# Hybrid diffusion backbone on one core: one of two groups of modulation pieces multiplied and summed on VectorE beside the projection, heads turned inside the context attention, six early gathers

## The reference, cut to what matters

```
def modulation(cvec, w_mod, b_mod):
    m = jax.nn.silu(cvec) @ w_mod + b_mod      # (1024,) @ (1024, 6144) + (6144,)
    return jnp.split(m, 6, axis=-1)
...
for i in range(DEPTH):
    mx = modulation(c, w_mod[i], b_mod[i]); mc = modulation(c_ctx, w_mod[i], b_mod[i])
    hx = modulate(rmsnorm(x, norm1[i]), mx[0], mx[1])
    hc = modulate(rmsnorm(h, norm1[i]), mc[0], mc[1])
    aq, ak, av, bq, bk, bv = split_cols(h @ w_in, EVEN_SIZES)   # then rmsnorm of q and k, rope
    ...                                  # attention, merge, out projection
    x = x + mx[5] * peer(...)            # 128 gathers of p_u and p_v rows per 128 tokens
```

## Time and profile before

| | us |
|---|---|
| median of 3 executions | 4426.19 (4411.77 to 4430.12) |
| the profiled execution, its own time | 4407.58 |
| its span in the profile | 4406.3 |
| TensorE busy | 3757.3 (85%) |
| VectorE busy | 2603.1 (59%) |
| ScalarE busy | 1746.1 (40%) |
| GpSimd busy | 1689.1 (38%) |
| mean granted clock of TensorE | 0.962 |

### The profile page before, as it was taken

How to read it: one execution, slowest core, us unless ns; L and a number is a source line. 1 busy time by engine, 2 the same in 40 slices (tenths; PEclk the granted TensorE clock), 3 DMA queues, 4 the chain that set the end, 5 groups by cost and what they waited for, 6 DMA issues and landing times. The chain is left out here.

```text
span 4406.3 us, 44443 instructions
## 1 busy us (share of the span) xinstructions
PE 3757.3 (85%) x12678; PEld 1911.6 (43%) x12678; DVE 2603.1 (59%) x5667; ACT 1746.1 (40%) x5137; POOL 1689.1 (38%) x1350
## 2 busy tenths in 40 slices
PE   5988789899998899878999966787989997877787
PEld 2444644555554445433444422556444552222222
DVE  3524687667866855676644433436766558666554
ACT  1112255555554444443333322322664433333333
POOL 0100144444444443444545412001444534656665
PEclk9989999999999999999999987899999999999999
DMA  4255899999999999999999971028999999999998
GB/s 174 108 212 198 288 424 401 412 419 424 404 425 426 426 420 426 427 391 427 427 427 427 427 295 37 4 86 297 394 372 412 425 423 405 427 427 427 427 427 363
DMA packets 248572, 1562.74 MB, mean 355 GB/s; under 512 B 30851, under 2 KB 44963, under 8 KB 77190
## 3 DMA queue, kind: packets, MB, share of 16 engines
q0 software_dynamic: 185088, 1342.36, 73.1%
q1 hardware_dynamic: 61014, 213.99, 12.9%
q10 hardware_dynamic: 2224, 3.55, 0.2%
HBM read 1551.43 MB, written 8.36 MB: 354 GB/s over the span
## 5 line engine op out<-in xcount | busy, mean ns | idle before, releaser
L2823 PE MATMUL ps<-ring,ex_diag 128*128 128x512 f32 x5120 | 2476.7, 618 | 416.6 <-ACT ex_diag L2812 389.7
L1586 POOL DMA_INDIRECT ring<-in_p_uv,expert x1280 | 1633.8, 1276 | 2179.3 <-PE ps L2823 1447.4
L2787 DVE SCALAR_TENSOR_TENSOR ring<-ring,H 128x1024 f32<-128x1024 f32 x1280 | 1557.5, 1225 | 1084.0 <-DMA ring<-in_p_uv,expert 1041.2
L2823 PEld LDWEIGHTS ps<-ring,ex_diag 128*128 128x128 f32 x5120 | 923.9, 194 | 1663.6 <-ACT ex_diag L2812 847.5
L2806 ACT ACTIVATE ex_act_w<-ex_dots 128x1 f32<-128x1 f32 x1280 | 258.1, 202 | 1471.4 <-DVE ring L2787 1465.2
L2812 ACT ACTIVATE ex_diag<-ident_sb,ex_weight 128x128 f32<-128x128 f32 x1280 | 513.9, 402 | 91.6 <-issue 3.1
L2808 ACT ACTIVATE ex_weight<-ex_act_w,gates 128x1 f32<-128x1 f32 x1280 | 377.1, 295 | 91.3 <-issue 4.2
L532 PE MATMUL ps<-win_w,hT 128*128 128x512 f32 (+1 forms) x480 | 191.9, 557 | 1.9 <-PEq L283 1.4
L532 PEld LDWEIGHTS ps<-win_w,hT 128*128 128x128 f32 x480 | 90.3, 191 | 106.0 <-issue 103.9
L1945 PEld LDWEIGHTS ps<-hTc,bs_w 128*128 128x128 f32 x768 | 110.8, 191 | 29.3 <-issue 23.5
L1945 PE MATMUL ps<-hTc,bs_w 128*128 128x128 f32 (+1 forms) x768 | 120.3, 310 | 0.3 <-issue 0.3
(11 more groups left out here) (456 smaller groups left out, 3314.6 us busy)
## 6 DMA issues: line engine op xcount, KB each, us to landing
ring<-in_p_wqk SPq DMA_DIRECT2D x64, 576.0 KB, 4.8
bs_w<-in_p_wqk SPq DMA_DIRECT2D x64, 576.0 KB, 8.0
ca_mod_w<-in_w_mod SPq DMA_DIRECT2D x24, 1024.0 KB, 9.5
ring<-in_p_uv,expert POOLq DMA_INDIRECT x1280, 13.9
win_mod_w<-in_w_mod SPq DMA_DIRECT2D x16, 1024.0 KB, 4.8
bs_w<-in_e_w_out_tiles SPq DMA_DIRECT2D x24, 512.0 KB, 8.0
win_w<-in_e_w_in SPq DMA_DIRECT2D x9, 1024.0 KB, 8.9
mod_mod_w<-in_w_mod SPq DMA_DIRECT2D x8, 1024.0 KB, 14.8
```

Of the source, the lines that this page charges most:

```text
L1586: pool.indirect_dma_start(m.ring[:, r, :], None, a["p_uv"], bass.IndirectOffsetOnAxis(ap=m.expert[:, t % 2, slot % SLOTS:slot % SLOTS + 1] ...
L2787: dve.scalar_tensor_tensor(out=ring[:, r, 0:D], in0=ring[:, r, 0:D], scalar=1.0, in1=h_of(t + t0), op0=ALU.mult, op1=ALU.mult, accum_out=d ...
L2823: mm = pe.matmul(mix_banks(t)[:, half, :], diag[:, b, :], ring[:, r, D + half * BANK:D + (half + 1) * BANK], start=(n == 0), stop=(n == SL ...
```

## The change

There are four edits.

- Group 2 of layer 0's modulation leaves TensorE. The new class `ModulationSums` has VectorE multiply each 128 x 2048 piece by the stream's coefficient (one a partition) and add it to an accumulator of the same size, for both streams: 16 instructions and as many drains, two after each of the VectorE steps 2, 5, ... 23 (`SUM_AT, SUM_GAP = 2, 3`). TensorE sums the accumulators over the partitions with eight matmuls against `m.sel` after unit 27. ScalarE issues the eight loads and four bias loads; the piece's buffer and the accumulators lie in `Hn`. One buffer: each load waits for both additions of the piece before. `Modulation` in this stage keeps group 1 alone, 8 pieces, `MOD_AT` is still 14, so they follow units 14 to 21.
- `turn_heads` is gone as a stage. The new class `Turns` turns the 8 parts of the context tiles at the start of the context attention, in eight banks, and TensorE waits for all their copies. The 16 parts of the latent tiles are turned at slots 3 + 6 n and copied by ScalarE at slots 5 + 6 n, all through PSUM bank 1; part n waits for the copy of part n - 1.
- The modulation in the context attention has bank 0 alone, so the first piece of a group waits for VectorE's four additions of the group before, and its 24 pieces are spread over the first 88 slots of 102.
- `EARLY` goes from 4 to 6, in both layers. `w_q` keeps three buffers in ring slots 6 and 7 and gets its fourth in memory of its own.

The core of the diff:

```diff
+class ModulationSums:
+    COLS = 4
...
+    def load(self, queue, k):
+        if k:
+            queue.wait_ge(self.used, 2 * k)
+        queue.dma_start(self.w, self.a["w_mod"][self.layer, self.group, k]).then_inc(self.loaded, 16)
...
+    def add(self, eng, k, stream):
+        coef, acc = self.m.csil[:, k, 2 + stream:3 + stream], self.acc[stream]
+        eng.wait_ge(self.loaded, 16 * (k + 1))
+        if k == 0:
+            add = eng.tensor_scalar(acc, self.w, coef, None, ALU.mult)
+        else:
+            add = eng.scalar_tensor_tensor(out=acc, in0=self.w, scalar=coef, in1=acc, op0=ALU.mult, op1=ALU.add)
+        add.then_inc(self.used, 1)
+        eng.drain()
+
+    def reduce(self, pe):
+        pe.wait_ge(self.used, 2 * KC)
+        for stream in range(2):
+            for j in range(self.COLS):
+                part, _ = self.chunk(j)
+                mm = pe.matmul(self.m.ps[part, self.bank, :], self.m.sel[:, 2 * stream:2 * stream + 2],
+                               self.acc[stream][:, j * BANK:(j + 1) * BANK], start=(stream == 0), stop=(stream == 1))
+        mm.then_inc(self.reduced, 1)
...
-    MOD_AT = NU - mods.pieces
+    MOD_AT = NU - 2 * mods.pieces
+    SUM_AT, SUM_GAP = 2, 3
...
+                    if u == NU - 3:
+                        on_dve.reduce(pe)
...
+                on_dve.load(act, 0)
                 for u in range(NU):
+                    if u > SUM_AT and (u - SUM_AT) % SUM_GAP == 2 and (u - SUM_AT) // SUM_GAP + 1 < KC:
+                        on_dve.load(act, (u - SUM_AT) // SUM_GAP + 1)
...
+                    if u >= SUM_AT and (u - SUM_AT) % SUM_GAP == 0 and (u - SUM_AT) // SUM_GAP < KC:
+                        for stream in range(2):
+                            on_dve.add(dve, (u - SUM_AT) // SUM_GAP, stream)
...
                 for g in range(len(mods.groups)):
                     mods.vector(dve, g)
+                on_dve.vector(dve)
...
                 mods.store(pool)
+                on_dve.store(pool)
...
+class Turns:
...
+    def begin_tensor(self, pe):
+        for n, part in enumerate(self.first):
+            self.turn(pe, part, n).then_inc(self.turned, 1)
+        for q in range(2):
+            pe.wait_ge(self.copied[q], len(self.first) // 2)
...
+    def tensor(self, pe, slot):
+        for n in self.at["turn"](slot):
+            if n:
+                pe.wait_ge(self.rest_copied, n)
+            self.turn(pe, self.rest[n], self.bank).then_inc(self.rest_turned, 1)
...
-        mods = Modulation(m, a, s, 1, [0, 1, 2], 8, (0, 1))
+        mods, turns = Modulation(m, a, s, 1, [0, 1, 2], 8, (0,)), Turns(m, s, 1)
...
-        steps = [slots * n // mods.pieces for n in range(mods.pieces)]
+        steps = [(slots - 14) * n // mods.pieces for n in range(mods.pieces)]
...
-EARLY = 4
+EARLY = 6
...
-                    pre, mods = InWeights(m, a, s), Modulation(m, a, s, 0, [1, 2], 2, (4, 5))
+                    pre, mods = InWeights(m, a, s), Modulation(m, a, s, 0, [1], 2, (4,))
...
-                turn_heads(nc, m)
```

More of the change, by code:

```diff
@@ L169, in vector @@
             part, _ = self.chunk(g, j)
-            dve.tensor_tensor(self.row[part, g % 2], self.m.ps[part, self.banks[g % 2], :], self.bias[part, g % 2], ALU.add)\
+            dve.tensor_tensor(self.row[part, g % 2], self.m.ps[part, self.banks[g % len(self.banks)], :], self.bias[part, g % 2], ALU.add)\
                 .then_inc(self.row_ready, 1)
@@ L465, in prefetch, with project_heads @@
             self.load(sp, n)
-def project_heads(nc, m, a, pre, mods):
+def project_heads(nc, m, a, pre, mods, spare):
     ORDER = pre.ORDER
@@ L491, in project_heads @@
     with Stage(nc, "ph0") as s:
+        on_dve = ModulationSums(m, a, s, "dve", 0, 2, spare[:, 2, :], [spare[:, n, :] for n in range(2)], 5)
         sq, ss = s.sb("sq", [P, 2, BANK]), s.sb("ss", [P, 2, 8])
@@ L633, in _ @@
                 mods.store(pool)
[L636 to L665, removed]
@@ L873, in _ @@
             def _(pe):
+                turns.begin_tensor(pe)
                 for slot in range(slots):
@@ L877, in _ @@
                             mods.tensor(pe, n)
+                    turns.tensor(pe, slot)
                     for h in heads:
@@ L882, in _ @@
             def _(dve):
+                turns.begin_copy(dve, dve.tensor_copy, 1)
                 for slot in range(slots):
@@ L898, in _ @@
             def _(act):
+                turns.begin_copy(act, act.copy, 0)
                 for slot in range(slots):
+                    turns.scalar(act, slot)
                     for h in heads:
@@ L1602, in first_choice @@
     with Stage(nc, f"fc{layer}") as s:
-        w_o = m.ring[:, 0:EARLY, :].rearrange("p r d -> p (r d)").rearrange("p (k d) -> p k d", d=D)
-        w_q = m.ring[:, EARLY:, :].rearrange("p r d -> p (r d)")[:, 0:RING * (KC + 1) * P].rearrange("p (r d) -> p r d", r=RING)
+        w_o = m.ring[:, 0:KC // 2, :].rearrange("p r d -> p (r d)").rearrange("p (k d) -> p k d", d=D)
+        behind = m.ring[:, EARLY:, :].rearrange("p r d -> p (r d)")
+        w_q = [behind[:, r * (KC + 1) * P:(r + 1) * (KC + 1) * P] for r in range(RING - 1)] + [s.sb("w_q", [P, (KC + 1) * P])]
         gate, gain, scale, shift_row = (s.sb(x, [P, D]) for x in ("gate", "gain", "scale", "shift_row"))
```

73 lines of the change are left out of this document (65 added, 8 removed).

## The result

| | us |
|---|---|
| before, median of 20 executions | 4411.07 (4402.62 to 4431.52) |
| after, median of 20 executions | 4428.27 (4421.99 to 4443.7) |
| ratio, with its 95% interval | 1.0041 [1.0031, 1.0051] |
| span of the profiled execution after | 4431.2 |
| mean granted clock of TensorE after | 0.963 |

The kernel became 17 us slower, where 26 us less were forecast. The front of the kernel came out nearly as predicted; the time was lost where the prediction had said that nothing would change.

The account below looks back on a forecast made before the run. It took gather bytes to bound the two expert stages and something else the front. Terms -23.8 + 2 - 4.9 + 1 = -25.7, say -26, from 4426.2 gave 4400 us; range 4392 to 4408, with rivals 4380 to 4416.

Parts of the forecast that it names:

- The step that failed: Two expert stages: limited by the bytes their gathers move, so a change ahead shifts them without changing their length.
- the sign that would refute it: Expert stages: the prediction is wrong if they change their length by more than 5 us.
- The projection: Projection stage: seven pieces fewer on TensorE, eight reduction matmuls more; end at 272 against 285.67, 13.7 us earlier.
- the "slower" rival: Projection: VectorE becomes the bound; TensorE stands from additions of 3.6 us, 4438 at 6 us; chance 0.03.
- The turns' start: Start of context attention: turns stage goes, first piece at 278.3 against 302.07, 23.8 us earlier, the projection's 13.7 contained.
- Inside the context attention: Context attention: added turns, bank waits and thinner tail +8, higher clock 6 back; sum +2, bounds -6 and +12.
- The tail: Last value of context attention to first_choice: only copy and stage end remain, 1.9 us against 6.76, 4.9 us earlier.
- EARLY: Seam into the experts: two more gathers move the stage end back 4.9 us; +1 for both layers, bounds +9.8 and -8.
- The experts' end stay: Expert stages: with two more early gathers the idle 4 us of DMA move along unfilled, so byte count and end stay.
- the two bounds: Early gathers: +9.8 if the delay shows in both layers, -8 if the stage end waits for something else, gaps filled.
- The whole: Whole kernel: -23.8 + 2 - 4.9 + 1 = -25.7, say -26, giving 4400; chance 0.62.
- The low clock in there: Context attention: first 20 us at 0.6 clock, bank wait whole; +12 in place of +2, time 4410; chance 0.17.

## Why the prediction was wrong, point by point

**The step that failed** is the one that was taken without a price: "they are limited by the bytes that their gathers move, and a change ahead of them shifts them without changing their length". Their limit is bytes at a rate, and the rate was taken as fixed. It depends on where the ring lies, and a tensor of 16 bytes ahead of it in the list of allocations moved the ring by 32. Measured alone, this is +43 us, of at most 52; in the changed kernel it is 44 (4428.27 - 4383.98). That -26 + 43 gives just the +17 that was measured is partly luck: the edits by themselves brought 27 to 32, and the place cost 44 to 46 on top of them. The prediction named the sign that would refute it ("if the expert stages change their length by more than 5 us"), and the stages changed by 34; it had no rival and no chance for it. The row to look at was in the list of allocations and not in the trace: the diff's core, as I had cut it, left the line with `m.sel` out.

The Trainium skill has a rule near this one, page "DMA: Bandwidth & Descriptors", section "How a descriptor splits into AXI transactions": a DMA descriptor (here one row) is cut into transactions of 256 bytes, and each must start on a 256-byte boundary; when the descriptor starts elsewhere, its first transaction starts at the boundary below, and the bytes in between cost beats (of 32 bytes) too. By it a row of 8192 bytes that starts 32, 64 or 128 bytes behind a boundary takes 33 transactions in place of 32 (3%), and 257, 258 or 260 beats in place of 256 (0.4, 0.8 and 1.6%; counting the thirty-third transaction as a full one would give 264, 3%). All of these are estimates by the page. That the boundary is at 256 agrees with the runs. The size doesn't: measured are 1.6, 1.4 and 1.2% for the three distances, less than the transactions and not growing as the beats. And the page speaks of what a descriptor reads, not of the place in SBUF, the memory on the chip, that it writes. Shown is that the ring's place decides, and that 32, 64 and 128 bytes off are slow where 0, 256 and 512 are not; why is open.

**The projection: right.** Last unit's end at 272.6 for 271.2, first turn at 273.31 for 272, where 1.4 us of the difference is there from unit 8 on (115.50 for 114.06), ahead of any piece. It is older than the stage: the projection's first matmul is at 72.34 for 70.67. Of these 1.7 us, 0.8 are there when the first transposes of the normalised tiles begin (56.53 for 55.74), and 0.9 are the last group of these, which took 1.97 us for 1.10; none of it is in an instruction that the change touches. TensorE never waits for VectorE in the projection. The additions, VectorE by line and form:

```profile
L216 DVE SCALAR_TENSOR_TENSOR Hn<-Hn,csil 128x2048 f32<-128x2048 f32 x14 | 32.9, 2349 | 0.9
L214 DVE TENSOR_SCALAR Hn<-Hn,csil 128x2048 f32<-128x2048 f32 x2 | 2.6, 1286 | 0.2
```

2.35 us, for 2.29 taken from another operation of that size; the "slower" rival needed 3.6 to begin. The 13.7 us forecast for the stage were measured as 12.4 from 285.67 to 273.31, 13.8 without those 1.4; as 13.6 at the first piece of the context attention against the kernel without the sums; and as 16 in the medians.

**The turns' start: right.** First piece at 279.89 for 278.3; less the 1.4 that came from before, 0.2 off.

**Inside the context attention: mis-sized.** From 279.89 to 375.34 are 95.45 us, before 85.5: +9.9, for +2 within bounds of -6 and +12. Its windows after:

```profile
278.00:302.00 24.00, 20.90 (x106) 8.02 (x107) 8.05 (x26) 6.69 (x23) 0.00 (x0) 0.86 1.01 417
302.00:326.00 24.00, 20.62 (x129) 8.68 (x128) 12.99 (x36) 8.99 (x32) 2.08 (x4) 1.00 1.01 417
326.00:345.00 19.00, 17.94 (x74) 7.91 (x73) 6.60 (x19) 4.69 (x16) 2.05 (x4) 0.55 0.59 244
345.00:365.00 20.00, 18.07 (x117) 9.32 (x115) 9.69 (x32) 8.89 (x30) 2.02 (x4) 1.00 0.01 1
365.00:375.30 10.30, 9.20 (x32) 6.61 (x32) 2.06 (x9) 3.93 (x12) 0.03 (x1) 0.52 0.01 1
```

The clock is higher at the start, as I had argued: a mean of 0.86 for 0.59 (each window is a mean of two levels, 1.00 and 0.5, that is 2.4 and 1.2 GHz). But it then falls twice, 326 to 345 at 0.55 and again in the last 10 us. Before, it was low once more, in a window that the rows left out:

```profile
338.00:347.00 9.00, 6.75 (x32) 2.77 (x32) 3.46 (x10) 2.47 (x10) 0.00 (x0) 0.81 0.92 365
```

An estimate from these rows, as if all busy time went with the clock: 20.90 busy us at 0.86, 17.94 at 0.55 and 9.20 at 0.52 would be 18.0, 9.9 and 4.8 at 1.00, so the low clock costs 15.4 us, where before 19.32 busy us at 0.59 and 6.75 at 0.81 cost 7.9 and 1.3. So some 6 of the +9.9 are the clock and the rest the turns' work. The kernel without the sums on VectorE has the same turns and the same spread of pieces, and one row of its windows and its last value are

```profile
326.00:345.00 19.00, 17.16 (x107) 7.77 (x99) 8.70 (x28) 7.03 (x25) 0.00 (x0) 1.00 1.01 425
382.18 1.97 PE L830 MATMUL ps<-KV,ca_probsT 128*128 128x64 f32 x8 [0.68 <-ACT ca_probsT L917]
```

There the fall in the middle doesn't come, and from 293.49 to 384.15 are 90.7 us: +5.2 for +9.9. So the turns alone don't bring the fall; these are single executions. What brings the clock down at 328 is open: TensorE was busy 86% of the 24 us ahead of the window, all at 1.00, and 94% of the 19 us at 0.55. In the two kernels with `m.sel` placed so that the ring is aligned, the same window has 0.58 and 0.64, so this isn't from the ring.

The waits of TensorE in this stage after:

```profile
PE ps L842 <- ACT ca_probsT L929: 4.4, 7, 1.0
PE ps L159 <- DMA ca_mod_w<-in_w_mod: 3.5, 1, 3.5
PE ps L159 <- DVE ca_mod_row L170: 1.9, 2, 1.0
PE ps L854 <- ACT ca_sunk L944: 1.4, 1, 1.4
```

The wait for ScalarE's copies falls from 7.9 to 4.4, which fits turns that fill 3.5 us of it (the forecast's reading; no run has the turns alone). The one bank costs 1.9 us, for 2, and 3.0 in the kernel with `m.sel` behind `m.eps`.

**The tail: right, a little better.** From the last value's end to `first_choice` 0.8 us, for 1.9 and 6.76 before: 6.0 us for 4.9.

**EARLY: right in mechanism.** The seam comes 1.7 and 2.2 us after the bytes of four and six gathers are in. From the end of the last early gather's issue to the next stage's first row are 13.6 us in the changed kernel, 11.8 in the one with `m.sel` behind `m.eps` and 12.3 in the kernel before with six, for 12 forecast and 9.6 before. "The experts' end stay" held in the kernel after, where four and six give the same time; alone in the kernel before it brought 7 us (0.998 [0.9965, 0.9995]), so of the two bounds +9.8 is excluded there and -8 is not.

**The whole:** -26 was forecast for the edits, and with the ring aligned they bring 27 to 32 us (4383.98 to 4381.79 against 4411.07; by the ratios 0.9925 to 0.9934 29 to 33). The profiled execution of the kernel with every edit at the addresses of before shows less, 18 us against that of before; of the 9 us between 18 and 27, 3.5 are the distance by which the profiled execution of before lies under its median (4407.58 for 4411.07) and 5.6 that by which the other lies above its own (4389.56 for 4383.98). The forecast of 4400 itself stood on a median of three executions, 4426.2; the median of twenty is 4411.07, and 26 less is 4385. So the sum was good to some us, and 4400 would have been 16 to 18 too high without the ring's shift. The 8 us too few inside the context attention are seen in the traces, and the medians don't tell whether something else made them up. The low clock in there, of which the prediction made a rival, is some 6 us of the case; the ring's place is 43 to 46.

## What to carry to other kernels

Where a stage runs on the rate of its gathers, read the plateau's GB/s after every change before anything else, and put the address of each buffer that gathers fill beside the diff: a tensor of a few bytes allocated ahead of it can cost more than the edit brings (43 us against some 30 here). Pad in front of such a buffer to a multiple of 256 bytes, or take a small tensor's room from one whose allocation already has it; both were measured here, with rows of 8192 bytes. And "this stage isn't touched" is a step of the sum that needs its row like any other.

## What the runs showed of the hardware that I had not expected

- Gathers of 128 rows of 8192 bytes ran at 427 GB/s into a ring that begins on a multiple of 256 bytes in the partition, and at 420 to 422 with an offset of 32, 64 or 128 bytes, with the DMA engines busy 1.01 in either case: 1.2 to 1.6% of rate, 38 to 43 us in 4411. The busy share of the DMA engines in the plateau doesn't show it; the GB/s do.
- Moving all other buffers by 32 bytes, those of VectorE, ScalarE and TensorE among them, changed nothing that can be measured (1.0008 [0.9988, 1.0028]).
- TensorE's granted clock fell to a mean of 0.55 in the midst of a stretch in which it was busy 94% of the time, and came back to 1.00 in the next 20 us, busy 90%. In the same window it had 0.55, 0.58, 0.64 and 0.64 in the four kernels with the sums on VectorE, and 1.00 in the one without them, one execution each. The cause is not settled.
